# Latent-attention keys: from a token-major projection with transposes to a channel-major projection with 64-column weights

## Reference

```python
kv = (rms_norm(ckv, g_kvn) @ w_ukv).reshape(B, n, 8, 64 + 64)     # w_ukv is 256 x 1024
kn, v = kv[..., :64], kv[..., 64:]
kr = apply_axial_rope(kr[:, :, None], cos, sin)[:, :, 0]          # 32 wide, one for all heads
s = einsum('bqhd,bkhd->bhqk', qn, kn) + einsum('bqhd,bkd->bhqk', qr, kr)
```

## Time and profile before

| | |
|---|---|
| median of 3 executions | 4365.72 us (4363.5 to 4368.82) |
| the profiled execution | 4371.33 us |
| its span, first to last instruction | 4369.6 us |
| PE busy / granted clock | 4143.0 us (95%) / 0.972 of full |
| DVE, ACT busy | 1442.3 us (33%), 1047.1 us (24%) |
| projection stages | about 61 to 350 us and 2372 to 2664 us of the span |

### The profile page before, as it was taken

The page is one execution under the profiler, slowest core; times in us unless marked ns, Lnnn a source line. Parts: engine busy times, 40 slices in busy tenths (PEclk is TensorE's granted clock), DMA queues, the critical chain, the costliest instruction groups (busy, mean ns, idle before and its releaser), DMA issues.

```text
span 4369.6 us, 67491 instructions
## 1 busy us (share of the span) xinstructions
PE 4143.0 (95%) x26108; PEld 2996.5 (69%) x26108; DVE 1442.3 (33%) x3473; ACT 1047.1 (24%) x2394; POOL 201.2 (5%) x229
## 2 busy tenths in 40 slices
PE   8999999999999699999999999999999968999995
PEld 4556667655545599999997555667544438999995
DVE  1235656522224411111112445656522361111113
ACT  1225555400012111111111324555300120000001
POOL 0000000000000000000000000000000000000002
PEclk9999999999999799999999999999999989999997
DMA  5121000322244888888886221000211538999994
GB/s 204 51 65 33 16 16 15 116 68 68 67 167 177 275 260 258 254 257 260 259 259 188 73 73 45 16 9 15 77 35 43 178 115 257 311 315 308 315 308 155
DMA packets 563037, 653.48 MB, mean 150 GB/s; under 512 B 19668, under 2 KB 494388, under 8 KB 562856
## 3 DMA queue, kind: packets, MB, share of 16 engines
q1 hardware_dynamic: 548504, 605.77, 42.9%
q0 software_dynamic: 14352, 45.23, 4.5%
HBM read 580.08 MB, written 70.86 MB: 149 GB/s over the span
## 4 chain that ended last, share of the span: by engine, by line
PE 83%; DVE 3%; issue 2%; DMA 1%; DVEq 1%; SPq 1%; ACT 0%; POOL 0%; POOLq 0%; ACTq 0%
PE PS L645 53%; PE PS L649 7%; PE PS L804 7%; PE PS L974 5%; PE PS L862 3%; PE PS L855 2%; PE PS L782 2%; PE PS L1130 1%; DVE arena L1430 1%; SPq L372 1%; PE PS L660 1%; PE PS L868 1%; DVE arena L1818 1%; DVEq L1823 0%; PE PS L789 0%
## 5 line engine op out<-in xcount | busy, mean ns | idle before, releaser
L645 PE MATMUL PS<-arena 128*128 128x160 f32 (+4 forms) x13344 | 2679.4, 363 | 18.4 <-DMA arena<-in_w_in 5.5
L645 PEld LDWEIGHTS PS<-arena 128*128 128x128 f32 x13344 | 1993.6, 191 | 678.9 <-issue 572.2
L1430 DVE TENSOR_TENSOR arena<-arena,PS 128x512 f32<-128x512 f32 (+3 forms) x444 | 202.2, 461 | 1172.0 <-ACT arena L1408 937.2
L649 PEld LDWEIGHTS PS<-arena 128*128 128x128 f32 (+1 forms) x3074 | 372.4, 142 | 282.1 <-issue 217.0
L649 PE MATMUL PS<-arena 128*128 128x128 f32 (+1 forms) x3074 | 472.0, 280 | 39.5 <-DMA arena<-x_mid,arena 17.4
L1408 ACT ACTIVATE arena<-PS 128x160 f32<-128x160 f32 (+1 forms) x256 | 74.5, 291 | 1372.3 <-PE PS L645 1372.3
L804 PE MATMUL PS<-arena 96*128 96x512 f32 (+1 forms) x800 | 363.3, 536 | 15.0 <-issue 13.1
L1430 DVE TENSOR_TENSOR arena<-arena 128x2 f32<-128x2 f32 (+10 forms) x421 | 227.3, 547 | 312.3 <-PE PS L645 234.3
L974 PE MATMUL PS<-arena 128*128 128x512 f32 x576 | 261.4, 609 | 13.8 <-POOL arena L1988 9.2
L1248 ACT ACTIVATE arena<-PS 128x256 f32<-128x256 f32 (+1 forms) x408 | 199.2, 489 | 257.1 <-PE PS L649 245.9
L1581 DVE TENSOR_REDUCE arena<-PS 128x1 f32<-128x512 f32 (+1 forms) x384 | 231.2, 603 | 76.8 <-PE PS L804 71.6
(11 more groups left out here) (186 smaller groups left out, 1851.6 us busy)
## 6 DMA issues: line engine op xcount, KB each, us to landing
arena<-in_w_exp_down SPq DMA_DIRECT2D x128, 1024.0 KB, 5.5
arena<-in_w_exp_gate SPq DMA_DIRECT2D x128, 1024.0 KB, 5.3
arena<-in_w_exp_up SPq DMA_DIRECT2D x128, 1024.0 KB, 7.8
arena<-in_w_ada SPq DMA_DIRECT2D x24, 2048.0 KB, 16.6
arena<-in_w_in SPq DMA_DIRECT2D x32, 512.0 KB, 5.4
h_transposed<-arena SPq DMA_DIRECT2D x20, 512.0 KB, 4.4
x_mid<-arena SPq DMA_DIRECT2D x18, 512.0 KB, 2.7
moe_sum<-arena SPq DMA_DIRECT2D x18, 512.0 KB, 3.7
```

The costliest lines, as they stand in the source:

```text
L645: m = pe.matmul(o, lt, rh, start=start and i == 0, stop=stop and i == n - 1)
L649: return pe.transpose(o, i, ident)
L1430: return dve.tensor_tensor(o, x, y, op)
```

## The change

The values of all eight heads are now one product (bank 6, moving columns picked in runs of 64). The keys are computed as channels by tokens: for each head the 64 key columns of `w_ukv` are the stationary operand and the 128 latent columns `latTt` move; even heads land in PSUM rows 0 to 63, odd heads in rows 64 to 127 of bank 5. The token-major buffer `ksb`, its eight transposes and its copies go. The rotated shared key `krr` is turned once, by a matmul with the identity into rows 64 to 95 of bank 1, and DVE copies it to all eight heads of `kT`. The core of the diff:

```diff
 # PE
-    mms(PS[:, 6, :], [(latTt[:, k, :], w_ukv[:, k, 512:1024]) for k in range(2)])
+    mms(PS[:, 6, :], [(latTt[:, k, :], w_ukv[:, k, :].rearrange("p (h c) -> p h c", c=NOPE + MV)[:, :, NOPE:]) for k in range(2)])
     (wait h_d, h_a of the next tile)
-    mms(PS[:, 5, :], [(latTt[:, k, :], w_ukv[:, k, 0:512]) for k in range(2)])
+    for i in range(4):
+        for k in range(2):
+            for g in range(2):
+                c0 = (2 * i + g) * (NOPE + MV)
+                m = pe.matmul(PS[g * 64:(g + 1) * 64, 5, i * P:(i + 1) * P], w_ukv[:, k, c0:c0 + NOPE], latTt[:, k, :], start=k == 0, stop=k == 1)
...
-    tr(PS[:, 1, 0:P], rW[:, 8:10, :]).then_inc(s["tW"], 1)
+    tr(PS[:, 1, 0:P], rW[:, 8:10, :])
     pe.wait_ge(*s("kr", t + 1))
-    pe.wait_ge(*s("kn", t + 1))
-    for g in (1, 0):
-        for h in range(4):
-            m = tr(PS[0:MQ, 5 + g, h * P:(h + 1) * P], ksb[:, g * 4 + h, :])
-        m.then_inc(s["tK"], 1)
+    pe.matmul(PS[64:96, 1, P:2 * P], krr, ident, start=True, stop=True).then_inc(s["tW"], 1)
 # ACT
-    for each half: copy 4 heads of values to V, 4 heads of keys to ksb
+    A(V[:, ds(t, 1), :].rearrange("p o n -> p (o n)"), PS[:, 6, :], ACT.Copy)
+    for g in range(2):
+        A(kT.rearrange("p (a b) t -> p a b t", b=2)[0:NOPE, :, g, ds(t * P, P)], PS[g * 64:(g + 1) * 64, 5, :].rearrange("p (a t) -> p a t", a=4), ACT.Copy).then_inc(s["kT_cp"], 1)
     (wait tW, qWs copy)
-    for i, g in enumerate((1, 0)):
-        act.wait_ge(*s("tK", 2 * t + i + 1))
-        A(kT[0:MQ, g * 4:(g + 1) * 4, ds(t * P, P)], PS[0:MQ, 5 + g, :]..., ACT.Copy).then_inc(s["kT_cp"], 1)
 # DVE
-    rope(krr ...).then_inc(s["used_d"], 1)
-    dve.drain()
-    (wait tK of the last tile)
-    dve.tensor_copy(ksb[:, :, NOPE:], krr.unsqueeze(1).to_broadcast([P, MH, ROPE])).then_inc(s["kr"], 1)
+    rope(krr ...).then_inc(s["kr"], 1)
     (queries: copies, rotations, qro)
     dve.wait_ge(*s("tW", t + 1))
+    dve.tensor_copy(kT[NOPE:MQ, :, ds(t * P, P)], PS[NOPE:MQ, 1, P:2 * P].unsqueeze(1).to_broadcast([ROPE, MH, P]))
     dve.tensor_copy(kaT[:, ds(t * P, P)], PS[:, 1, 0:P]).then_inc(s["ka_cp"], 1)
```

More of the change, by code:

```diff
@@ L66, in layer_counts @@
     n |= {k: 16 * TT for k in "x_in h_st qW_st qM_st".split()}
-    n |= {k: TT for k in "h_a h_d p1 p2 p0 rms rstd norm latT latc_a latc_d used_d ropeW kr kn qro tW qW_cp ka_cp".split()}
-    n |= {k: 2 * TT for k in "xT ukv uq tK tQ kT_cp qM_cp".split()}
+    n |= {k: TT for k in "h_a h_d p1 p2 p0 rms rstd norm latT latc_a latc_d ropeW kr qro tW qW_cp ka_cp".split()}
+    n |= {k: 2 * TT for k in "xT ukv uq tQ kT_cp qM_cp".split()}
     n |= dict(mrg=KD * chunks, g=KD * (5 + chunks), sg=KD * (4 + chunks), gsum=KD * 5, ss=KD * 2 + 2)
@@ L149, in build @@
         latTt = at(R + 19840, 5, P)
-        ksb = at(R + 20480, MH, MQ)
         qsb = at(R + 21248, MH, MQ)
@@ L703, in step @@
                         pe.wait_ge(*s("norm", t))
-                        pe.wait_ge(*s("used_d", t))
                         pe.wait_ge(*s("ka_cp", t))
@@ L731, in step @@
                     pe.wait_ge(*s("wu_in", 16 * 2))
-                    mms(PS[:, 6, :], [(latTt[:, k, :], w_ukv[:, k, 512:1024]) for k in range(2)]).then_inc(s["ukv"], 1)
+                    mms(PS[:, 6, :], [(latTt[:, k, :], w_ukv[:, k, :].rearrange("p (h c) -> p h c", c=NOPE + MV)[:, :, NOPE:]) for k in range(2)]).then_inc(s["ukv"], 1)
                     if not last:
@@ L735, in step @@
                         pe.wait_ge(*s("h_a", t + 2))
-                    mms(PS[:, 5, :], [(latTt[:, k, :], w_ukv[:, k, 0:512]) for k in range(2)]).then_inc(s["ukv"], 1)
+                    for i in range(4):
[3 more added lines that the diff above has]
+                                m = pe.matmul(PS[g * 64:(g + 1) * 64, 5, i * P:(i + 1) * P], w_ukv[:, k, c0:c0 + NOPE], latTt[:, k, :], start=k == 0, stop=k == 1)
+                    m.then_inc(s["ukv"], 1)
                     pe.wait_ge(*s("latc_d", t + 1))
@@ L764, in _ @@
                 pe.wait_ge(*s("ka_cp", TT))
-                pe.wait_ge(*s("used_d", TT))
                 def scores(p, lp, n, part):
@@ L1202, in step @@
                         h_half(t + 1)
-                    for i, g in enumerate((1, 0)):
[L1205 to L1211, removed]
+                    act.wait_ge(*s("ukv", 2 * t + 1))
+                    A(V[:, ds(t, 1), :].rearrange("p o n -> p (o n)"), PS[:, 6, :], ACT.Copy)
+                    act.wait_ge(*s("ukv", 2 * t + 2))
+                    for g in range(2):
+                        A(kT.rearrange("p (a b) t -> p a b t", b=2)[0:NOPE, :, g, ds(t * P, P)], PS[g * 64:(g + 1) * 64, 5, :].rearrange("p (a t) -> p a t", a=4), ACT.Copy).then_inc(s["kT_cp"], 1)
                     act.wait_ge(*s("tW", t + 1))
@@ L1215, in step @@
                     A(qWs.rearrange("p a b -> p (a b)"), PS[:, 7, :], ACT.Copy).then_inc(s["qW_cp"], 1)
-                    for i, g in enumerate((1, 0)):
-                        act.wait_ge(*s("tK", 2 * t + i + 1))
-                        A(kT[0:MQ, g * 4:(g + 1) * 4, ds(t * P, P)], PS[0:MQ, 5 + g, :].rearrange("p (h c) -> p h c", h=4), ACT.Copy).then_inc(s["kT_cp"], 1)
                 tiles(act, step)
@@ L1540, in step @@
                     rope(rW, src, tab[:, 0:128], 10, 16, rC).then_inc(s["ropeW"], 1)
-                    rope(krr.unsqueeze(1), PS[:, 2, QR:QR + ROPE].unsqueeze(1), tab[:, 128:192], 1, 8, krt.unsqueeze(1)).then_inc(s["used_d"], 1)
-                    dve.drain()
-                    if not (isinstance(t, int) and t == 0):
-                        dve.wait_ge(*s("tK", 2 * t))
-                    dve.tensor_copy(ksb[:, :, NOPE:], krr.unsqueeze(1).to_broadcast([P, MH, ROPE])).then_inc(s["kr"], 1)
+                    rope(krr.unsqueeze(1), PS[:, 2, QR:QR + ROPE].unsqueeze(1), tab[:, 128:192], 1, 8, krt.unsqueeze(1)).then_inc(s["kr"], 1)
                     if not (isinstance(t, int) and t == 0):
```

## The result

The changed kernel takes 4391.35 us in the median of 6 executions (4389.47 to 4394.66), the kernel before 4366.09 us in 6 (4363.5 to 4369.25). The ratio is 1.0058 with a 95% interval of 1.0047 to 1.0069: slower by 25.3 us. The direction and the mechanism were forecast, the size was not: 11.7 us were forecast, and 4391.35 lies above the range's end of 4384.

The account below looks back on a forecast made before the run. PE was taken to bound the kernel, with DVE mattering where its results come late. Normal boundaries 10.2, kv_only boundaries 0.3 and stage ends 1.2 gave +11.7 us on 4365.7: 4377.4 us, range 4369 to 4384.

Parts of the forecast that it names:

- Rival A: At the tile's end DVE's new copy is hidden, under about 0.7 us: 4367.9 us in total; chance 0.16.
- B: Before the query transposes DVE is ahead, so the removed transposes' price is kept: faster, 4356.4 us; chance 0.05.
- C: In the key product the halves don't overlap: +1.72 us a tile, 4412 us; chance 0.03.
- The +0.52 of part 3: DVE's new 1.21 us copy to kT delays ka_cp and the next tile's first load by 0.52 us.
- Operations start 0.08 before their forerunner's end: On DVE at the tile's end, the new copy and the next start 0.08 us before the preceding operation ends.
- The +0.02 and +0.10 of part 1: Key product on PE, per tile: 0.02 us for 32 narrow instructions, 0.10 for the width change (bounds 0 and 0.21).
- the step into K lies under the 0.6 us wait for L1508: Entering the half-width key product is covered by PE's wait for DVE, except in a layer's last tile.
- The two kv_only boundaries: After kv_only tiles DVE is the chain; removing L1545 gives back 0.38 us, leaving 0.14 each, 0.3 together.
- K's terms are hidden: At the boundaries after kv_only tiles, the key product's extra PE costs add nothing, since DVE is the chain.
- The clock: Clock after the stage ends, where PE restarts after a pause: named as a possible difference in the total, without a size.
- The stage ends: At each layer's projection end L1562 ends 0.46 us later; with the key product's costs 0.58 each, 1.2 for two.
- rival D: Width change costs its upper 0.21 us and the copy 1.37: 4382 us; chance 0.76 together with the forecast.

Follow-up runs that it names:

- e4: e3 with the key product issued after the query expansion instead of before it; 4365.33 us, 0.9995 of the kernel before.
- e7: Changed kernel with the key product's loops turned, all even heads and then all odd heads; 4419.97 us in one execution.
- e1: Changed kernel with the turned rotary key in bank 0 and its DVE copy behind the query copies, with its own count; 4376.28 us, 1.0020.
- e2: Changed kernel with key columns of w_ukv packed in front by the load, so a pair of heads is one full-width product; 4391.81 us, 1.0056.
- e3: Changed kernel with both the edits of e1 and e2; 4377.8 us, 1.0020 of the kernel before.
- e5: Changed kernel, half-width keys and contiguous load kept, keys issued after the query expansion, turned key in bank 0 and copied by ACT; 4361.52 us, 0.9992.
- e6: e4 with the copy to kT on ACT and the packed weights loaded behind the constants (layer 0) or first kept rows (layer 1); 4362.12 us, 0.9991.

## Why the prediction was wrong

The chain was right: PE's work hardly changes, the removed transposes give nothing because `qro` sets the start of `tQ` (wait 0.73, forecast "about 0.8"), the copy for eight heads makes `ka_cp` late. Rival A fails, since the copy took 1.22 us and isn't hidden. B fails as an account of this change, though e4 shows that the price it names was there. C fails by e7. What failed are sizes.

**The +0.52 of part 3** measured 0.81, the largest miss. The copy itself was right within 0.01. The step that failed is "Operations start 0.08 before their forerunner's end": copied from neighbours of the kind in the earlier trace rows, it didn't hold round the new copy (0.03 after, 0.02 after), and "0.05 later as after `qro`" was 0.11. Why the overlap is absent there stays open; it goes with this copy: in e1 it is back between the rotation and the window key copy, and the moved copy again starts 0.03 after its forerunner's end (134.07+1.28 = 135.35, then 135.38). 16 x 0.29 = 4.6 us. (The forecast also looked for the wait on PEld; the trace shows it on PE, 0.6 us, and on PEld as 0.79 us of "issue".)

**The +0.02 and +0.10 of part 1** measured 0.31, of which 0.24 to 0.26 go with the half-width form (e2 against the changed kernel, e3 against e1, e5 against e4 and e6) and 0.06 with the number of instructions (e2). The pitch was right: 0.051 us, 32 loads in 1.73. The last narrow load starts about 127.08+31x0.051 = 128.66 and the first wide one at 128.97, 0.31 later where 0.05 to 0.11 would do. The bound of 0.21 from the earlier trace rows was the better value than the 0.10 taken. And "the step into K lies under the 0.6 us wait for L1508" failed: the first narrow load comes 0.17 after the end of L1500 (126.91), the wide one of the earlier trace rows came 0.05 after, so 0.12 is added behind the wait and not under it. By e2, e3 and e5 the round trip costs about 0.25 us here. The Trainium skill's rule (TensorEngine Tiling (Array Packing), section Key Properties) that a change of tiling mode drains the engine fits both, though no run looks inside the engine. 16 x 0.19 = 3.0 us.

**The two kv_only boundaries**, "0.52-0.38 = 0.14 each", measured 1.0 and 1.5: from the first transpose of the stage to tile 1's first product 25.88 us became 26.89 (2369.96 to 2395.84, 2374.90 to 2401.79), and from there to tile 2's 22.14 became 23.62. "K's terms are hidden" was the wrong step: the value products ran partly at the low clock, and the narrow ones couldn't begin until they were done, so PE, not DVE, set L1539 (it waits 0.56 us for L644 in tile 0, 0.96 in tile 1). This kept L1545's removal from giving the 0.38. That the low clock and the narrow form share the rest is read from the loads; no run separates them.

**The clock** was named as a place where the total could differ, at the stage ends; it came in layer 1's tile 2, 1.6 us, which had no term. What decides on it stays open: it is absent in the kernel before, e1, e4, e5 and e7 and present in the changed kernel, e2, e3 and e6, in which tile 1 ran anything but alike (21.8 us in e3 and e6, 23.6 in the changed kernel).

**The stage ends**, forecast at 0.58 each, came to about 1.04: from tile 9's first load to the first score load layer 1 took 31.88 us before (2632.31 to 2664.19) and 32.92 after (2649.27 to 2682.19; both starts are tile 8's mark plus the 0.94 and 0.40 us by which the load follows it); layer 0 shows the same two lengths. Of it 0.66 lies behind `qro`'s end (0.46 forecast; DVE's looser handovers) and 0.38 ahead of it (0.12 forecast). Tile 9 has no wait for h_d: its first narrow load comes 0.95 us behind the last wide one, where a wide one came after 0.43.

The account: 16 x 1.12 = 17.9 for the normal boundaries (10.2 forecast), 2.5 for the context tiles (0.3), 2.1 for the ends (1.2), 1.6 for the clock (0): 24.1 against 11.7. The remaining 1.2 us of the measured 25.3 are below what the runs tell apart.

The bound also had a mistake of form: rival D, the highest sum under the range's end of 4384, took upper bounds for two terms alone. Three more handovers (the copy's start, the next copy's start, PE's load), each repeated 16 to 18 times, were all off the same way, since each was taken as the tightest one seen.

## What to carry to other kernels

Before counting a removed instruction as a gain, look who waits behind it: here 0.64 us of PE work a tile went and became a longer wait on DVE (0.18 to 0.73 us), and only reordering (keys behind queries) turned it into 0.5 us. A small copy placed in front of a count that the next iteration needs is paid in full on every pass; give its source a bank that nobody reuses soon, or put the copy on the idle engine. Price a changed tile width by its exit and entry, not by its pitch, and a repacked weight load by who is queued behind it: one late start of 3.1 to 3.4 us took back most of the 4.8 us that 20 tiles gained.

## What the runs showed of the hardware

- 64-column products in alternating halves come every 0.051 us, in one half every 0.095 us, full-width ones of 128 moving columns every 0.108 us. Nearly the whole gain is the alternation.
- Going to half width and back costs about 0.25 us a tile beyond the pitch (e2, e3, e5). The first narrow load starts only about when the wide products ahead end (2395.10 against 2395.17; in tile 9 349.41 against 349.48), 0.37 and 0.52 us later than a wide load in its place.
- DVE's copy of 1024 elements from PSUM on 32 partitions took 1.22 us, ACT's 1.01 us.
- DVE's usual start 0.08 us before the end of the operation ahead was missing on both sides of that copy: 0.03 and 0.02 us after the end.
